# Feed-forward inputs left unscaled by the norm's root, sums of squares inside the first groups, weight splits in their place: a two-layer hybrid decoder on one core

## The reference, cut to what matters

```python
def rms_norm(x, gain=None):
    y = xf * lax.rsqrt(jnp.mean(xf * xf, axis=-1, keepdims=True) + EPS)
    ...
def swiglu(x, w_in, w_out):
    gate, up = jnp.split(x @ w_in, 2, axis=-1)
    return (jax.nn.silu(gate) * up) @ w_out
...
    h = x + 0.5 * rms_norm(swiglu(rms_norm(x, p['n_ffn1_pre']), ...), p['n_ffn1_post'])
    m, ... = token_mixing(rms_norm(h, p['n_mix_pre']), ...)
    h = h + rms_norm(m, p['n_mix_post'])
    h = h + 0.5 * rms_norm(swiglu(rms_norm(h, p['n_ffn2_pre']), ...), p['n_ffn2_post'])
```

## Time and profile before

| | |
|---|---|
| median of 3 runs | 1949.99 us (1949.07 to 1951.47) |
| the profiled execution | 1949.37 us, of it a span of 1947.6 us |
| PE busy | 1852.9 us, 95% of the span, 16354 matmul records |
| DVE busy | 1290.5 us, 66% |
| ACT busy | 894.6 us, 46% |
| POOL busy | 119.9 us, 6% |
| chain that ended last | PE 71%, DVE 16%, issue 6%, ACT 5%, DMA 2% |
| mean granted TensorE clock | 0.991 of full |

### The profile page before, as it was taken

The page is one execution under the profiler, slowest core; times in us unless marked ns, Lnnn a source line. Parts: engine busy times, 40 slices in busy tenths (PEclk is TensorE's granted clock), DMA queues, the critical chain, the costliest instruction groups (busy, mean ns, idle before and its releaser), DMA issues.

```text
span 1947.6 us, 40532 instructions
## 1 busy us (share of the span) xinstructions
PE 1852.9 (95%) x16354; PEld 1784.8 (92%) x16354; DVE 1290.5 (66%) x1902; ACT 894.6 (46%) x1023; POOL 119.9 (6%) x176
## 2 busy tenths in 40 slices
PE   6999999999998998999989999999999899989997
PEld 6899999988888998999989999998888899989997
DVE  5656577758767867665575656767676776776554
ACT  4433354456564353433344334465566435353333
POOL 0000001101210100000000000010111010000000
PEclk9999999999999999999999999999999999999999
DMA  7676656666764555565667765776676554556653
GB/s 234 185 206 190 181 171 226 215 214 217 249 212 146 181 177 191 163 184 164 181 186 204 208 175 162 222 230 202 222 236 207 181 179 152 188 164 189 175 170 112
DMA packets 436074, 372.47 MB, mean 191 GB/s; under 512 B 9474, under 2 KB 413316, under 8 KB 435010
## 3 DMA queue, kind: packets, MB, share of 16 engines
q1 hardware_dynamic: 411728, 278.76, 48.0%
q0 software_dynamic: 24160, 91.12, 13.8%
HBM read 343.16 MB, written 26.69 MB: 190 GB/s over the span
## 4 chain that ended last, share of the span: by engine, by line
PE 71%; DVE 16%; issue 6%; ACT 5%; DMA 2%; DVEq 0%; SPq 0%; ACTq 0%
PE proj L634 47%; PE proj L657 4%; PE proj L652 4%; PE proj L653 4%; DVE wl L1677 2%; ACT wh L1238 1%; DVE qkvt L2027 1%; PE aux L684 1%; DVE y L1831 1%; PE aux L1009 1%; PE aux L852 1%; DVE sring L2094 1%; PE aux L1055 1%; DVE x L1850 1%; DVE y L1849 1%
## 5 line engine op out<-in xcount | busy, mean ns | idle before, releaser
L1677 DVE TENSOR_TENSOR wl<-raw,wh 128x2048 fp32r<-128x2048 f32 (+1 forms) x282 | 603.8, 2141 | 213.2 <-ACT wh L1238 193.3
L1238 ACT CAST wh<-raw 128x2048 fp32r<-128x2048 f32 (+1 forms) x282 | 503.8, 1787 | 435.7 <-PE proj L634 296.1
L634 PE MATMUL proj<-xh,wh 128*128 128x264 f32 x2688 | 391.3, 288 | 8.0 <-ACTq L1335 7.9
L634 PE MATMUL proj<-xl,wh 128*128 128x264 f32 x2688 | 391.2, 286 | 2.0 <-DVEq L1806 2.0
L634 PE MATMUL proj<-xh,wl 128*128 128x264 f32 x2688 | 381.4, 285 | 3.6 <-DVE wl L1677 3.5
L634 PEld LDWEIGHTS proj<-xl,wh 128*128 128x128 f32 x2688 | 350.9, 189 | 16.4 <-issue 13.2
L634 PEld LDWEIGHTS proj<-xh,wh 128*128 128x128 f32 x2688 | 350.0, 189 | 11.2 <-ACTq L1335 5.0
L634 PEld LDWEIGHTS proj<-xh,wl 128*128 128x128 f32 x2688 | 348.0, 189 | 5.8 <-DVE wl L1677 5.8
L653 PE MATMUL proj<-hl,wh 128*128 128x264 f32 x704 | 173.3, 283 | 0.0
L652 PE MATMUL proj<-hh,wh 128*128 128x264 f32 x704 | 173.0, 283 | 0.0
L652 PEld LDWEIGHTS proj<-hh,wh 128*128 128x128 f32 x704 | 132.4, 188 | 0.0
(11 more groups left out here) (431 smaller groups left out, 2242.7 us busy)
## 6 DMA issues: line engine op xcount, KB each, us to landing
raw<-ffn_w_in SPq DMA_DIRECT2D x176, 512.0 KB, 5.1
raw<-w_in SPq DMA_DIRECT2D x80, 1024.0 KB, 5.6
raw<-ffn_w_out SPq DMA_DIRECT2D x64, 704.0 KB, 4.6
sring<-cache_mem_k POOLq DMA_DIRECT2D x32, 512.0 KB, 5.1
sring<-cache_mem_v POOLq DMA_DIRECT2D x32, 512.0 KB, 4.3
out<-sring POOLq DMA_DIRECT2D x32, 512.0 KB, 4.4
sring<-state_gdn POOLq DMA_DIRECT2D x32, 512.0 KB, 5.2
raw<-w_mem_v SPq DMA_DIRECT2D x10, 1024.0 KB, 6.3
```

The costliest lines, as they stand in the source:

```text
L634: mm = pe.matmul(o, w[:, s, k * 256 + t * P:k * 256 + (t + 1) * P], a[:, k, :], **go)
L1238: act.copy(wh[:, slot, 0:size], raw[:, slot, 0:size]).then_inc(hi_done[slot], 1)
L1677: dve.tensor_sub(wl[:, slot, 0:size], raw[:, slot, 0:size], wh[:, slot, 0:size].bitcast(F32)).then_inc(split_done[slot], 1)
```

## The change

What it does, by engine:

- PE: `total` of the outer norm no longer follows the last product group but stands in the middle of the first memory group (`mid`, after its tile t = 0). In front of `f1i` and `f2i`, `square_total` moves from between the two memory groups into the first feed-forward group, whose parts are now ordered high t0, high t1, low weights t0, low weights t1, sum of squares, low input t0, low input t1 (`late_low`). In `mk` it moves from behind group 0 to the middle of group 2.
- ACT: the splits held back are made in their place, ahead of the root. In front of the feed-forward, `xh = x * gain` comes straight from `x` (`gained_high`, 4 activations for a half), ahead of the squares, and the root is taken in the first feed-forward group. Silu works on `gate` in SBUF, in place (`gated_hidden`), after DVE has filled it (`product_scaled`).
- DVE: `xl = x * gain - xh` (`gained_low`). `hidden_tile` multiplies both product tiles by the reciprocal of the root, the gate tile before Silu and the up tile after it, so each feed-forward group has two more DVE operations, and PSUM is freed by them.
- In `mk` the norm of the mixing input is still applied to the input; its parts move behind groups 1 and 2.

The diff, cut to its core:

```diff
+                    if late_low and i == u == 0:
+                        for part in (HIGH, WEIGHT_LOW, INPUT_LOW):
+                            for t in range(2):
+                                if part == HIGH:
+                                    pe.wait_ge(bank_free[t], bank_use(l, ph, i, u, t) + 1)
+                                elif part == WEIGHT_LOW and t == 0:
+                                    pe.wait_ge(split_done[s], n + 2)
...
+                            if part == WEIGHT_LOW:
+                                late_low()
...
-                products(l, "mvb", memh, meml, "natural", groups=(0,))
-                square_total(l, 1)
-                products(l, "mvb", memh, meml, "natural", groups=(1,))
-                products(l, "f1i", xh, xl, early=halves(1))
+                products(l, "mvb", memh, meml, "natural", mid=last_result)
+                products(l, "f1i", xh, xl, early=halves(1), late_low=lambda: square_total(l, 1))
                 products(l, "f1o", hh, hl, early=hidden_tiles(0))
-                total(l, "p1", "sqp")
-                products(l, "mk", memh, meml, groups=(0,))
-                square_total(l, 2)
-                products(l, "mk", memh, meml, groups=(1, 2, 3))
+                products(l, "mk", memh, meml, mid=key_norm)
...
-                total(l, "p2", "sqp")
-                products(l, "mva", memh, meml, "natural", groups=(0,))
-                square_total(l, 3)
-                products(l, "mva", memh, meml, "natural", groups=(1,))
-                products(l, "f2i", xh, xl, early=halves(3))
+                products(l, "mva", memh, meml, "natural", mid=mixed_result)
+                products(l, "f2i", xh, xl, early=halves(3), late_low=lambda: square_total(l, 3))
...
+            def gated_hidden(l, which, summed):
+                def tile(ph, i, u):
+                    j = 4 * i + u
+                    if j == 0:
+                        root(l, summed, "rt")
+                    act.wait_ge(product_scaled, (2 * l + which) * FT + j + 1)
+                    order(act.activation(gate[:, u % 2, :], gate[:, u % 2, :], ACT.Silu))
+                    act.sem_inc(gate_ready, 1)
...
+                def gained_high(n):
+                    for half in range(2):
+                        x_wait(n, half)
+                        for k in range(4 * half, 4 * half + 4):
+                            order.apart(act.activation(xh[:, k, :], x[:, k, :], ACT.Copy, scale=gains[...]))
+                        order.wait()
+                        tell("xh_all" if half else "xh_half")
+                    for half in range(2):
+                        square_half(n, half)
...
-                stream(l, "out", squares(l), after=lambda g: tell("b1_done") if g == 0 else None, hold=True)
+                stream(l, "out", squares(l), after=lambda g: tell("b1_done") if g == 0 else None)
                 order.fresh()
-                result_root(2, "out")
-                squares_around(3, "mva", values(0))
+                root_table()
+                stream(l, "mva", values(0, (l, "p2")), groups=(0,))
+                gained_high(3)
                 stream(l, "mva", values(0), groups=(1,))
-                stream(l, "f2i", through(l, ACT.Silu, "first"))
+                stream(l, "f2i", gated_hidden(l, 1, "n3"))
...
-            def hidden_tile(l, first):
+            def hidden_tile(l, n):
                 def tile(ph, i, u):
                     j = 4 * i + u
+                    if j == 0:
+                        norm_wait(dve, l, "rt", n)
+                        order(dve.reciprocal(rt[:], rt[:]))
+                    bank = tile_wait(dve, l, ph, i, u, 0)
+                    order(tt(gate[:, u % 2, :], proj[bank][:, 0:T], rt[:], ALU.mult))
+                    dve.sem_inc(bank_free[bank], 1)
+                    dve.sem_inc(product_scaled, 1)
                     bank = tile_wait(dve, l, ph, i, u, 1)
+                    order(tt(tmpf[:], proj[bank][:, 0:T], rt[:], ALU.mult))
+                    dve.sem_inc(bank_free[bank], 1)
                     dve.wait_ge(gate_ready, l * ACT_TILES + GATE0[ph.name] + j + 1)
-                    order(tt(tmpf[:], proj[bank][:, 0:T], gate[:, u % 2, :], ALU.mult))
-                    dve.sem_inc(bank_free[bank], 1)
+                    order(tt(tmpf[:], tmpf[:], gate[:, u % 2, :], ALU.mult))
...
+                def gained_low(n):
+                    for half, name in enumerate(("xh_half", "xh_all")):
+                        norm_wait(dve, l, name, n)
+                        for k in range(4 * half, 4 * half + 4):
+                            order.apart(stt(xl[:, k, :], x[:, k, :], gains[...], xh[:, k, :].bitcast(F32), ALU.mult, ALU.subtract))
+                        order.wait()
+                        tell(f"xn{n}")
...
-                stream(l, "f1o", result_tile(l, 1, "sqp"), hold=True)
+                stream(l, "f1o", result_tile(l, 1, "sqp"))
                 add_result(1, "x2")
-                held_split(l, "f1o")
-                norm_x(2, 2, lambda: stream(l, "mk", groups=(0,)))
-                stream(l, "mk", groups=(1, 2, 3))
+                stream(l, "mk", groups=(0, 1))
+                norm_x(2, 2, lambda: stream(l, "mk", groups=(2,)))
+                stream(l, "mk", groups=(3,))
...
                 add_result(2, "x3")
-                held_split(l, "out")
-                norm_x(3, 4, lambda: stream(l, "mva", groups=(0,)))
+                stream(l, "mva", groups=(0,))
+                gained_low(3)
                 stream(l, "mva", groups=(1,))
```

159 lines of the change are left out of this document (86 added, 73 removed).

## The result

The changed kernel takes 1929.88 us, the median of 4 runs (1928.73 to 1932.03), beside 1950.73 us for the kernel before on the same chip (4 runs, 1949.07 to 1953.81): a ratio of 0.989, with a 95% interval of 0.9869 to 0.991. The forecast was 1931.0, its range 1925 to 1940. The profiled execution took 1930.05 us, with a span of 1928.3 at a mean clock of 0.990.

A forecast was written before the change was run, and what follows sets the result against it. PE bounds the kernel, busy 1852.9 of 1947.6 us, so only its 95 us idle can be won. 13.3 + 6.3 - 0.6 = 19.0 us won gives 1931.0, range 1925 to 1940.

The forecast's parts named there:

- The outer total: Five inner boundaries: PE reaches the total at about 2.9 us, the 1.85 us pause goes, the root is 2.1 later.
- In front of the feed-forward: Before `f1i` and `f2i`: one pause of about 2.1 us replaces six; 4.3, 4.2 and 4.8 won, together 13.3.
- restarts: Each PE pause costs 0.2 us beyond its listed idle time, weight load included; the bound was nothing.
- In front of `mq`: `f1o` to `mq`: pauses of 1.1 us for a low split and 0.3 for `xl`; 3.2 and 3.1 won, together 6.3.
- (e): A transfer lands late at a split no longer held, delaying the root 1 to 2 us at five boundaries: 1938; chance 0.05.
- Start of layer 0: First feed-forward: PE waits 3.9 plus 1.3 us where it waited 3.84 and 1.03; cost 0.6 with the restart.
- `f2o` to `f1i`: DVE has about 1 us of copies ahead of the split, which ends as PE needs it; 4.2 us won.
- Inside the feed-forward: 88 groups: ACT-DVE loop 5.3 us, DVE loop 5.0, both below 5.80, so two more DVE operations cost nothing.
- (a): Wait only moved: PE waits 4 us in front of `f2i`, 3 before `mq`; gain 9, so 1941; chance 0.10.
- (b): Half clock after each new pause and one more elsewhere: 8 us, so 1939; chance 0.09.
- (c): Feed-forward loop through ACT and DVE outgrows 5.80; breaks even at 6.0, 1957 at 6.1; chance 0.04.
- (d): ACT's table load dearer than listed: root 1.4 us later at five boundaries, 7 us less won, 1938; chance 0.02.

## Why the prediction was right, point by point

The time was right to 1 us, and so was its mechanism; some terms were off in both directions.

- **The outer total.** Forecast at 2.9 us after the last group, found at 767.05, 2.7 after; the root forecast from 4.8, found at 4.6; the reciprocal at 5.4, found at 5.3. The pause is gone at five boundaries. The copy of the memory tile stood in the forecast as 0.5 us ahead of the root. With the total in front that copy waits 1.70 us for PE, and the root with it; in the changed kernel it doesn't wait.
- **In front of the feed-forward.** One pause, of 1.88 us where 2.1 was forecast; four scaled copies take 1.74 where 1.7 was taken from the earlier trace rows; the squares are summed from 17.8 (forecast 17.9), and there is no wait for `xl`. Yet 5.1 us were won at the undisturbed boundary of layer 0 and not 4.3. The mis-sized term is the one put down to restarts. Idle time fell by 3.55 us (5.43 to 1.88), the busy time of the same matmuls by 1.54 (22.96, from the window 768.29 to 796.68 of before, to 21.42): a mean of 0.31 for each of the five pauses that went, where I had 0.2. It isn't the price of a pause, since the order of the parts changed too: the sum of squares takes 3.36 us from its start to the next part, and took 3.71 in two halves with the pause between them left out. Where one pause alone comes or goes, the busy time moves by less: by 0.03 with the total put back (21.42 to 21.45), and by 0.2 where the early split of `mk` takes away the one in front of `mq` (26.90 to 26.71).
- **In front of `mq`.** ACT in the changed kernel, behind `f1o` of layer 1 (end at 1184.94), then DVE's split:

```profile
1185.74 1.91 ACT L1261 CAST wh<-raw 128x2048 fp32r<-128x2048 f32 x1 [0.36 <-DMA raw<-w_mem_k]
```

```profile
1197.93 2.29 DVE L1715 TENSOR_TENSOR wl<-raw,wh 128x2048 fp32r<-128x2048 f32 x1
```

 The pause for the low split is 1.59 us where 1.1 was forecast: PE is there at 13.75 us after `f1o` in layer 1 (forecast 13.8), but the split ends at 15.3 and not at 14.9. The root comes at 5.1, 0.3 later than forecast and 0.5 later than in front of `f2i`; 0.2 of that is the split ahead of it, which waits 0.36 us for its transfer. That is rival (e), at a fifth of its price. The wait for `xl`, forecast at 0.3, is there with 0.23 in both layers, inside the first group of `mq` (the line at 1216.24 above). Up to the start of `mq` 3.4 us are won; behind that wait, where the forecast's 3.2 and 3.1 belong, 2.9 in both layers (37.69 less 34.83, and 37.66 less 34.78). What is short is the 0.5 of the low split.
- **Start of layer 0.** ACT's copies keep PE waiting 3.89 and then 0.54 us. The forecast had 1.3 for the second, 1.8 between the two halves of `xh` less 0.5 for four products. At the lower clock, at which PE runs there, four products are listed with 1.22 us and not with the 0.73 of other boundaries, and so hide more of the copies. That is 0.5 of the difference; the term was -0.6 and came out as 0.6, and the rest isn't accounted for beyond the restarts.

```profile
51.08 1.22 PE L626 MATMUL proj<-xh,wh 128*128 128x264 f32 x4 [3.89 <-ACTq L1367]
52.84 3.01 PE L626 MATMUL proj<-xh,wh 128*128 128x264 f32 x12 [0.54 <-ACTq L1367]
```

- **`f2o` to `f1i`.** 3.3 won instead of 4.2, with the cost that the bounds had named: a new stretch at half clock behind the pause at `xh`. The changed kernel, the window just behind it:

```profile
990.00:993.30 3.30, 3.30 (x17) 3.20 (x17) 3.15 (x9) 2.80 (x4) 0.56 (x1) 0.57 0.58 169
```

- **Inside the feed-forward.** The loop is 5.39 us where the rows gave 5.3, against PE's 5.80. The two experiments with added operations put the edge where the forecast put it: 5.86 costs some 5 us in all, 6.32 costs 8 to 10 us a phase. DVE's busy time rose by 58.6 us, and not by 66: the added gate scaling starts 0.08 before the listed end of the low split (815.90, with the split from 813.69 for 2.29), and 88 such overlaps are 7 us.
- **The rivals.** (a), a wait only moved, didn't happen here, but it is what the kernel with the splits held back does. (b) came at one of the three new pauses of 1.88 us in the first profile and at two of them in the second, so one in six was too low a share. (The six of before weren't equal either: five have 1.85 us and one 2.31, and behind the last of them, where PE has next to nothing to do, the clock falls too.) Each mixing stage lost 1.5 us, 0.5 of it the pause for `xl`. The rest is less than what can be named in it: in layer 1 a load that landed late, 2.24 us, in layer 0 a stretch at half clock at 618 us. `out` of layer 0 gained 1.4, for the stretch at 745 us of before isn't there. (c) would have needed a loop of 6.0, and the loop is 5.39.
- **(d), the table load.** Here it is followed by the next activation 0.02 us after its listed end (766.91 plus 1.28, then 768.21), and the root ends at 5.1 us. By the Trainium skill, "ScalarE: Activation LUTs", section "What ACT_TABLE_LOAD costs", a switch costs a drain of about 1.38 us beside the load. The trace of the changed kernel disagrees, as that of before did: ACT's split ends at 766.89, 0.02 us before the load, and the next activation follows it as closely. The root's time agrees with the rows.

The sum came out right partly by luck. The forecast left the mixing stages at 0; they lost 3.0 us between them, 1.0 of it the pauses for `xl` that the forecast had in front of `mq`, and `out` gave 1.4 back. The boundaries and the start gave 21.4 where 19.0 was forecast. Differences of 1 to 2 us from clock and loads are those of one execution. The second profile of the changed kernel won 17.6 us of span against the same profile of before: 1.4 instead of 0.6 at the start, 3.6 instead of 5.1 from `out` to `f2o` in layer 0, and -3.0 and 1.5 instead of -1.5 twice in the mixing phases, while `out` of layer 0 took 29.6 us instead of 26.8.

## What to carry to other kernels

Where several engines hand a norm around while the matrix engine works on something else, list every wait of one boundary, and ask of each edit what is late next: moving the sum, dropping the root from the input and giving the splits their places were worth 19 us together, about 12 without the first, and nothing without the second or without the third. Work that is put off behind an engine's long step (here the low split behind the residual add) comes back as a wait of nearly that step's length. Measure what an edit won at a point behind every wait that it can move: 1.8 us won in front of `mq` were 0.3 behind its first group. A pause costs its idle time, up to some 0.3 us of restart here, and in some cases a stretch at half clock behind it; what is added to an engine with idle time costs nothing only while the longest loop through it stays under the period of the engine that sets the pace.

## What the runs showed of the hardware that was not expected

- What a pause of PE costs beyond its idle time isn't one number. The same 163 matmuls, from `out` to the second group of `f2i`, were busy 22.96 us with six pauses, 21.42 with one and 21.45 with two; in front of `mq` one pause of 1.59 us made 0.2 us (26.71 to 26.90).
- Whether the clock falls behind a pause isn't set by its length alone, nor by the program. In the first profile of the changed kernel it fell behind the pause of 1.88 us in front of `f1i` of layer 1, with 17 matmuls in 3.3 us, and stayed at 1.00 behind those of the same length in front of both `f2i`; in the second it fell in front of `f2i` of layer 0 as well. Behind all nine pauses of 5.3 to 5.9 us at the boundaries of two experiments (splits held back, inputs scaled) it fell, to 0.50 to 0.59; behind one of 5.54 us at 14.6 us from the start it stayed at 1.00.
- The half-clock stretches move from one execution to the next. Two profiles of the same changed kernel, of 1928.3 and 1930.0 us, have them in different places of the mixing stage, and `out` of layer 0 took 26.8 us in one and 29.6 in the other.
- A dependent operation of 264 columns on DVE adds 0.46 us to a loop that runs over it, though it is listed with 0.43, and starts 0.08 before the listed end of a long one ahead of it.
